# Second attention of a two-block layer: the softmax weights are divided on GpSimd before they are transposed, and the output is written in channel order

## The chip, the cores and the metric

The kernel runs on one core of a Trainium2 chip. The metric is the device time of one execution in microseconds (us); lower is better. The engines are named as the profile names them: PE (TensorE matmul), PEld (TensorE weight load), DVE (VectorE), ACT (ScalarE), POOL (GpSimd), SP (SyncE).

## What is computed

A model of two blocks in float32 over 1024 tokens. The first block (attention, two state-space mixers, a feed-forward part) is untouched. The second block projects the normed input into queries (8 heads of 64), keys and values (2 heads of 64), a gate, and a gated second branch. The part that changes is its attention:

```
def one_block(q_blk):
    s = jnp.einsum('bhgqd,bhkd->bhgqk', q_blk, kt).astype(jnp.float32) * scale
    p = jax.nn.softmax(s, axis=-1).astype(vt.dtype)
    return jnp.einsum('bhgqk,bhkd->bhgqd', p, vt)
...
attn = block_attention(q, k, v) * jax.nn.silu(gate_a)
y_a = jnp.einsum('bse,ed->bsd', attn, w_proj_attn)
```

Queries go in 8 blocks of 128, four query heads share a key head, and `scale` is 1/8. Each query sees all 1024 keys.

## The kernel before

Every engine has its own program, and all of them walk one list, `schedule`, which fixes each engine's order; semaphores tie the engines together. float32 products are made exact enough by splitting an operand into a rounded part (hi) and the rest (low).

The second attention is one stretch of that list, from 1475 to 1698 us of the profile. Its unit is a **pair** of query heads in one block of 128 tokens: 8 blocks times 4 pairs, 32 pairs. For head-block n (64 of them, two for each pair m):

- `a2s`: PE makes the scores, 128 queries by 1024 keys, in two PSUM banks (L1686). DVE takes the row maximum (L2800) and multiplies it by -0.125 (L2801).
- `a2e`: ACT makes exp(0.125 x - 0.125 max) of the 1024 columns into one of four SBUF tiles `Pb`, with the row sum into `a2d` (L2152). The weights stay undivided.
- `a2x (m, q)`, q = 0 to 3: PE transposes a quarter of both heads' `Pb` into a side bank (4 transposes, L1695), ACT copies it to the hi part of `PT` (L2161), DVE makes the low part (L2244).
- `a2v (m, q)`: PE multiplies the quarter with the values, hi and low stacked on the 128 partitions (L1707). After q = 3 ACT copies the sum to `ovt` (L2167).
- `a2o m`: `fold` is two identities side by side. Two products with `ovt` as the stationary operand (L1719) add hi and low and give the output with the queries on the partitions. DVE inverts the two row sums (L2810) and multiplies the output with them into `ot` (L2812).
- `a2t c`, after every fourth pair: PE transposes the four 128-column pieces of `ot` (L1725), and DVE copies them to the channel-major `aoT` (L2816).

The stages of neighbouring pairs are interleaved: `a2x (m+1, 0)` and `(m+1, 1)` stand between the value products of pair m. POOL has no work in the stretch. In front of it stand the query blocks (`q2T`, `q2B`: rotation and norm on DVE, where the gains in `qkg` are folded into the rotation table) and the making of `fold` (L2779); behind it come the gate product on DVE (L2819), sums of activations (`c2`) and the next projections (`vi`).

PE's side products share four banks in turn. A result of each DVE instruction is waited for before the next one of that engine runs; the helper `step` does this on ACT and POOL too.

## Time and profile before

| | |
|---|---|
| median of 3 runs | 2219.86 us (2218.81 to 2220.01) |
| the profiled execution, its own time | 2217.14 us |
| its span | 2215.3 us |
| PE, PEld busy | 94%, 79% of the span |
| DVE, ACT, POOL busy | 59%, 43%, 45% |
| granted TensorE clock, mean | 0.98 of full speed |

The page's 40 slices of some 55 us show the second attention as slices 27 to 31:

```
DVE  4443605867348734434479696789997865225532
POOL 1333433543336788888830302210002469885344
GB/s 153 73 104 113 144 51 49 72 120 63 147 58 96 39 58 60 67 65 76 67 181 143 143 93 122 82 29 1 1 1 34 39 20 58 114 96 105 105 124 76
```

A digit is the busy share of a slice in tenths. The shares of the whole span mix stages with different limits; what the change touches is read from its own stretch. Times in a timeline are counted from the start of the span.

### The profile page before, as it was taken

How to read it: one execution, taken by the hardware profiler on the slowest of the kernel's cores; microseconds unless marked ns; L12 is line 12 of the kernel's file. 1: busy time of each engine (PE TensorE's matmuls, PEld its weight loads, DVE VectorE, ACT ScalarE, POOL GpSimd, SP SyncE). 2: the span in 40 equal slices, each digit the busy share in tenths (PEclk: the TensorE clock that was granted, in tenths of full speed). 3: DMA queues.
4: the chain of work that ended last, by engine and by line, in shares of the span. 5: the costliest groups of instructions: out<-in, count | busy, mean ns of one | idle time of the engine just before them, and what ended most of it. 6: DMA issues, size and time to landing. Idle time of an engine off the chain costs nothing. (4 is left out here: it accounts for less than half of the span.)

```text
span 2215.3 us, 30029 instructions
## 1 busy us (share of the span) xinstructions
PE 2084.4 (94%) x10653; PEld 1750.5 (79%) x10661; DVE 1303.4 (59%) x1945; ACT 947.8 (43%) x1679; POOL 991.2 (45%) x723
## 2 busy tenths in 40 slices
PE   6999999889998999999999978989999999999997
PEld 6888877778786788888888857768887888887886
DVE  4443605867348734434479696789997865225532
ACT  4332215565234433343455544247775444544012
POOL 1333433543336788888830302210002469885344
PEclk9999999999999999999999999999999999999999
DMA  4233412354512122222254423210001102333331
GB/s 153 73 104 113 144 51 49 72 120 63 147 58 96 39 58 60 67 65 76 67 181 143 143 93 122 82 29 1 1 1 34 39 20 58 114 96 105 105 124 76
DMA packets 185892, 179.49 MB, mean 81 GB/s; under 512 B 27556, under 2 KB 147088, under 8 KB 184336
## 3 DMA queue, kind: packets, MB, share of 16 engines
q1 hardware_dynamic: 157568, 107.51, 16.7%
q10 hardware_dynamic: 19216, 46.99, 5.7%
q0 software_dynamic: 8960, 23.07, 4.7%
q8 instruction: 86, 1.41, 0.3%
q14 instruction: 62, 0.51, 0.1%
HBM read 150.81 MB, written 49.81 MB: 91 GB/s over the span
## 5 line engine op out<-in xcount | busy, mean ns | idle before, releaser
L1206 POOL TENSOR_SCALAR w_hi<-w_raw 128x1024 fp32r<-128x1024 f32 x67 | 76.2, 1137 | 469.3 <-issue 310.0
L1348 PE MATMUL gemm<-h_hi,w_hi 128*128 128x512 f32 x688 | 271.8, 395 | 5.6 <-POOL h_lo L1260 5.6
L1350 PE MATMUL gemm<-h_hi,w_lo 128*128 128x512 f32 x688 | 268.2, 390 | 0.0
L1349 PE MATMUL gemm<-h_lo,w_hi 128*128 128x512 f32 x688 | 268.0, 390 | 0.0
L954 POOL TENSOR_TENSOR w_lo<-wsum,w_hi 128x512 fp32r<-128x512 f32 x160 | 214.7, 1342 | 102.6 <-ACT w_hi L1814 94.7
L1814 ACT ACTIVATE w_hi<-wsum 128x512 fp32r<-128x512 f32 x171 | 108.3, 633 | 183.9 <-POOL wsum L945 94.1
L954 POOL TENSOR_TENSOR w_lo<-w_raw,w_hi 128x512 fp32r<-128x512 f32 x86 | 116.3, 1353 | 138.7 <-ACT w_hi L1814 134.1
L1209 POOL TENSOR_TENSOR w_lo<-w_raw,w_hi 128x1024 fp32r<-128x1024 f32 x67 | 166.8, 2489 | 5.6
L1430 PE MATMUL gemm<-h_hi,w_hi 128*128 128x512 f32 x416 | 161.9, 389 | 0.0
L1431 PE MATMUL gemm<-h_lo,w_hi 128*128 128x512 f32 x416 | 161.8, 389 | 0.0
L1432 PE MATMUL gemm<-h_hi,w_lo 128*128 128x512 f32 x416 | 161.8, 389 | 0.0
L1348 PEld LDWEIGHTS gemm<-h_hi,w_hi 128*128 128x128 f32 x688 | 129.4, 188 | 34.2 <-issue 8.7
L1350 PEld LDWEIGHTS gemm<-h_hi,w_lo 128*128 128x128 f32 x688 | 129.3, 188 | 27.4
L1349 PEld LDWEIGHTS gemm<-h_lo,w_hi 128*128 128x128 f32 x688 | 129.5, 188 | 25.4
L945 POOL TENSOR_TENSOR wsum<-w_raw,w_raw 128x512 f32<-128x512 f32 x96 | 129.3, 1347 | 7.5
L1255 POOL TENSOR_TENSOR wt<-h_lo 128x512 f32<-128x512 f32 x12 | 18.9, 1574 | 232.9 <-DVE aoT L2819 228.1
L2275 DVE SCALAR_TENSOR_TENSOR cacc<-cin,cols,cacc 128x1024 f32<-128x1024 f32 x42 | 65.5, 1560 | 84.5 <-ACT cacc L1773 83.5
L2341 DVE TENSOR_TENSOR ca<-m,gemm 128x512 f32<-128x512 f32 x32 | 22.0, 687 | 146.4 <-ACT m L1883 146.4
L1814 ACT ACTIVATE w_hi<-w_raw 128x512 fp32r<-128x512 f32 x130 | 82.3, 633 | 48.9 <-PE gemm L1432 36.6
L1430 PE MATMUL gemm<-cmb,w_hi 128*128 128x512 f32 x240 | 94.1, 392 | 4.2 <-POOL w_lo L954 4.2
L2161 ACT ACTIVATE PT<-side 128x512 fp32r<-128x512 f32 x128 | 76.6, 599 | 43.6 <-PE side L1695 39.3
L2244 DVE TENSOR_TENSOR PT<-side,PT 128x512 fp32r<-128x512 f32 x128 | 88.5, 691 | 9.7 <-ACT PT L2161 5.8
(487 smaller groups left out, 5425.2 us busy)
## 6 DMA issues: line engine op xcount, KB each, us to landing
w_raw<-in_w_in SPq DMA_DIRECT2D x60, 512.0 KB, 3.9
down_sums<-in_ffn_w_down POOLq DMA_DIRECT2D x24, 768.0 KB, 7.2
w_raw<-in_ffn_w_gate SPq DMA_DIRECT2D x22, 512.0 KB, 3.9
w_raw<-in_ffn_w_up SPq DMA_DIRECT2D x22, 512.0 KB, 4.0
w_raw<-down_sums SPq DMA_DIRECT2D x44, 256.0 KB, 2.7
w_raw<-in_ffn_w_down SPq DMA_DIRECT2D x44, 256.0 KB, 2.8
w_raw<-in_w_out SPq DMA_DIRECT2D x16, 512.0 KB, 3.8
sig_spill<-quad ACTq DMA_DIRECT2D x5, 1024.0 KB, 3.8
```

Of the source, the lines that this page charges most:

```text
L945: step(ops.tensor_tensor(wsum[sum_of[n]["buf"]][:], x, y, op), "w_sum" if who == "pool" else "w_sum_v")
L954: ops.tensor_tensor(quarter(wlo, slot), x, quarter(whi, slot), ALU.subtract).then_inc(w_split, 1)
L1209: gp.tensor_tensor(lo[:], raw[key % 4][:], hi[:], ALU.subtract).then_inc(w_split, 1)
L1348: mm(o, hi[:, k, m], act[0][:, k, t], start=k == 0, stop=False)
L1349: mm(o, hi[:, k, m], act[1][:, k, t], start=False, stop=False)
L1350: last = mm(o, lo[:, k, m], act[0][:, k, t], start=False, stop=k == kt - 1)
L1430: mm(o, hi[:, k, :], b[0], start=k == 0, stop=False)
L1431: mm(o, hi[:, k, :], b[1], start=False, stop=False)
L1432: last = mm(o, lo[:, k, :], b[0], start=False, stop=k == 3)
L1814: step(af(quarter(whi, slot), x, ACT.Copy), "w_quarter_hi")
L2161: step(af(PT[q][0][:], b[:], ACT.Copy), "hi_ready")
L2244: ins = v.tensor_tensor(dst, b, hi, ALU.subtract)
```

## The change

- POOL multiplies each `Pb` tile in place by the inverse of its row sum, a column of `a2d` (64 instructions of 128x1024, new kind `a2e` in POOL's program). The inverse is made by DVE with one instruction for each head-block (`weight_scale`). PE's transposes of a pair wait for POOL's product of its second head instead of ACT's exponentials.
- `fold` is 64 columns wide and is now the stationary operand, `ovt` the moving one: each of the two products writes 64 output partitions, and the output comes out in channel order. DVE copies 128 columns straight into `aoT`. L2810 and L2812 go, and `a2t` goes with its transposes and copies.
- The query gain in `qkg` is multiplied by -0.125 once. The scores are then the negated scaled ones, DVE takes their minimum (one instruction, no L2801), and ACT computes exp(-x + min). The bias columns rotate over four instead of two.

Waits that named the last `a2t` now name the last `a2o`. Unused semaphores go, which changes no instruction.

```diff
-        s += [("a2t", m // 4 - 1)] * (m % 4 == 0 and m > 0) + [("a2o", m)]
-    s += [("a2t", NT - 1), ("load", 3)]
+        s.append(("a2o", m))
+    s.append(("load", 3))
...
-        fold = sbuf("fold", [P], 216)
+        fold = sbuf("fold", [64], 216)
...
-        ot = sbuf("ot", [512], 212)
...
-                        side_consumed(pool, (("a2t", NT - 1), 0))
+                        side_consumed(pool, (("a2o", 4 * NT - 1), 0))
                         pool.wait_ge(N["ga_gated"], 1)
                     if j >= 2:
                         pool.wait_ge(N["c2_s"], j - 1)
                     step(gp.tensor_tensor(wt[j % 2][:], hF[1][:, r1, t1], hF[1][:, r2, t2], op), "c2_w")
+                elif kind == "a2e":
+                    pool.wait_ge(N["p_scale"], j + 1)
+                    step(gp.tensor_scalar(Pb[j % 4][:], Pb[j % 4][:], a2d[:, j % 8:j % 8 + 1], None, ALU.mult), "p_normed")
                 elif kind == "norm" and j[0] == 1:
...
-                        scores_consumed(pe, 2 * m)
-                        scores_consumed(pe, 2 * m + 1)
+                        pe.wait_ge(N["p_normed"], 2 * m + 2)
...
-                        last = mm(b[:, hslice(i)], ovt[j % 2][:, hslice(i)], fold[:], start=True, stop=True)
-                    done(last, (it, 0))
-                elif kind == "a2t":
-                    side_consumed(pe, (("a2o", 4 * j + 3), 0))
-                    b = bank((it, 0))
-                    for i in range(4):
-                        last = tr(b[:, hslice(i)], ot[:, hslice(i)], ident)
+                        last = mm(b[64 * i:64 * i + 64, 0:P], fold[:], ovt[j % 2][:, hslice(i)], start=True, stop=True)
                     done(last, (it, 0))
...
-                    step.frees_scores(af(Pb[j % 4][:], g[:], ACT.Exp, bias=a2m[:, 2 + j % 2:3 + j % 2], scale=0.125,
+                    step.frees_scores(af(Pb[j % 4][:], g[:], ACT.Exp, bias=a2m[:, j % 4:j % 4 + 1], scale=-1.0,
                                          accum_out=a2d[:, j % 8:j % 8 + 1]), j)
...
+            def weight_scale(n):
+
+                if n < 2 * 4 * NT:
+                    scores_consumed(dve, n)
+                    d = a2d[:, n % 8:n % 8 + 1]
+                    step(v.reciprocal(d, d), "p_scale")
+
...
+                            step(v.tensor_scalar(g, g, -0.125, None, ALU.mult))
...
-                        for k in range(2):
-                            step(v.tensor_copy(fold[r, 64 * k:64 * k + 64], ident[r, r]), "fold_ready" if h and k else None)
+                        step(v.tensor_copy(fold[r, :], ident[r, r]), "fold_ready" if h else None)
...
-                    mx, neg = a2m[:, j % 2:j % 2 + 1], a2m[:, 2 + j % 2:3 + j % 2]
-                    step(v.reduce_max(mx, g[:], axis=AX))
-                    step(v.tensor_scalar(neg, mx, -0.125, None, ALU.mult), "a2_max")
+                    step(v.tensor_reduce(a2m[:, j % 4:j % 4 + 1], g[:], axis=AX, op=ALU.min), "a2_max")
                 elif kind == "a2x":
-                    q = j[1]
+                    m, q = j
+                    if j == (0, 0):
+                        weight_scale(0)
+                        weight_scale(1)
+                    if q == 2:
+                        weight_scale(2 * m + 3)
                     b = side_product(dve, (it, 0))
                     low(PT[q][1][:], b[:], PT[q][0][:], (it, 0))
+                    if q == 0:
+                        weight_scale(2 * m + 2)
                 elif kind == "a2o":
-                    h = 2 * j % 8
-                    for i in range(2):
-                        scores_consumed(dve, 2 * j + i)
-                    step(v.reciprocal(a2r[:], a2d[:, h:h + 2]))
                     b = side_product(dve, (it, 0))
-                    step.frees(v.tensor_tensor(h64(ot[:, h * 64:h * 64 + P]), b[:, 0:256].rearrange("p (h n) -> p h n", h=2)[:, :, 0:64],
-                                               widen(a2r[:], 64), ALU.mult), (it, 0))
-                elif kind == "a2t":
-                    b = side_product(dve, (it, 0))
-                    step.frees(v.tensor_copy(aoT[:, :, hslice(j)], b[:].rearrange("p (i n) -> p i n", i=4)), (it, 0))
+                    step.frees(v.tensor_copy(aoT[:, j % 4, hslice(j // 4)], b[:, 0:P]), (it, 0))
```

What that does to the order. DVE, in the middle of the stage, over a little more than one pair (`PT_1` is the low part, `PT_0` the hi part; the number behind is a buffer). Before:

```order
L2800 TENSOR_REDUCE a2m<-gemm 128x1 [waits gemm_done1,side_read0]
L2801 TENSOR_SCALAR a2m<-a2m 128x1 [waits dve_step]
L2244 TENSOR_TENSOR PT_1_275<-side,PT_0_274 128x512 [waits hi_ready,side_done1,a2_max]
L2244 TENSOR_TENSOR PT_1_277<-side,PT_0_276 128x512 [waits hi_ready,side_done2,side_read1]
L2800 TENSOR_REDUCE a2m<-gemm 128x1 [waits gemm_done3,side_read2]
L2801 TENSOR_SCALAR a2m<-a2m 128x1 [waits dve_step]
L2810 RECIPROCAL a2r<-a2d 128x2 [waits gemm_read1,gemm_read3,a2_max]
L2812 TENSOR_TENSOR ot<-side,a2r 128x128 [waits side_done3,dve_step]
L2244 TENSOR_TENSOR PT_1_279<-side,PT_0_278 128x512 [waits hi_ready,side_done0,side_read3]
L2244 TENSOR_TENSOR PT_1_281<-side,PT_0_280 128x512 [waits hi_ready,side_done2,side_read0]
```

After:

```order
L2801 TENSOR_REDUCE a2m<-gemm 128x1 [waits gemm_done1,side_read1]
L2239 TENSOR_TENSOR PT_1_275<-side,PT_0_274 128x512 [waits hi_ready,side_done2,a2_max]
L2295 RECIPROCAL a2d<-a2d 128x1 [waits gemm_read3,side_read2]
L2239 TENSOR_TENSOR PT_1_277<-side,PT_0_276 128x512 [waits hi_ready,side_done3,p_scale]
L2801 TENSOR_REDUCE a2m<-gemm 128x1 [waits gemm_done3,side_read3]
L2815 COPY aoT<-side 128x128 [waits side_done0,a2_max]
L2295 RECIPROCAL a2d<-a2d 128x1 [waits gemm_read1,side_read0]
L2239 TENSOR_TENSOR PT_1_279<-side,PT_0_278 128x512 [waits hi_ready,side_done1,p_scale]
L2239 TENSOR_TENSOR PT_1_281<-side,PT_0_280 128x512 [waits hi_ready,side_done3,side_read1]
L2801 TENSOR_REDUCE a2m<-gemm 128x1 [waits gemm_done1,side_read3]
```

What was L2244, L2800 and L2812 is now L2239, L2801 and L2815. The multiplications of the maximum are gone, one inverse stands behind the low part of quarter 0 and one ahead of the low part of quarter 2, each waiting for ACT's exponential (gemm_read), and the product with the inverse has become a copy.

DVE at the start of the stage, from the third row reduction on. Before:

```order
L2800 TENSOR_REDUCE a2m<-gemm 128x1 [waits gemm_done3,a2_max]
L2801 TENSOR_SCALAR a2m<-a2m 128x1 [waits dve_step]
L2800 TENSOR_REDUCE a2m<-gemm 128x1 [waits gemm_done1,a2_max]
L2801 TENSOR_SCALAR a2m<-a2m 128x1 [waits dve_step]
L2244 TENSOR_TENSOR PT_1_275<-side,PT_0_274 128x512 [waits hi_ready,side_done1,a2_max]
L2244 TENSOR_TENSOR PT_1_277<-side,PT_0_276 128x512 [waits hi_ready,side_done2,side_read1]
```

After:

```order
L2801 TENSOR_REDUCE a2m<-gemm 128x1 [waits gemm_done3,a2_max]
L2801 TENSOR_REDUCE a2m<-gemm 128x1 [waits gemm_done1,a2_max]
L2295 RECIPROCAL a2d<-a2d 128x1 [waits gemm_read3,a2_max]
L2295 RECIPROCAL a2d<-a2d 128x1 [waits gemm_read1,p_scale]
L2239 TENSOR_TENSOR PT_1_275<-side,PT_0_274 128x512 [waits hi_ready,side_done1,p_scale]
L2295 RECIPROCAL a2d<-a2d 128x1 [waits gemm_read3,side_read1]
L2239 TENSOR_TENSOR PT_1_277<-side,PT_0_276 128x512 [waits hi_ready,side_done2,p_scale]
```

The first two inverses stand behind the fourth row reduction, and with them all that follows from them.

POOL at the same place. Before:

```order
L1206 TENSOR_SCALAR w_hi_55<-w_raw_53 128x1024 [waits raw_loaded2,gemm_done1,w_split]
L1209 TENSOR_TENSOR w_lo_57<-w_raw_53,w_hi_55 128x1024 [waits pool_hi]
L1255 TENSOR_TENSOR wt_294<-h_lo 128x512 [waits ga_gated,side_read0,w_split]
L1255 TENSOR_TENSOR wt_295<-h_lo 128x512 [waits c2_w]
```

After (`Pb` in place, with a column of `a2d`):

```order
L1205 TENSOR_SCALAR w_hi_55<-w_raw_53 128x1024 [waits raw_loaded2,gemm_done1,w_split]
L1208 TENSOR_TENSOR w_lo_57<-w_raw_53,w_hi_55 128x1024 [waits pool_hi]
L1257 TENSOR_SCALAR Pb_270<-Pb_270,a2d 128x1024 [waits p_scale,w_split]
L1257 TENSOR_SCALAR Pb_271<-Pb_271,a2d 128x1024 [waits p_scale,p_normed]
L1257 TENSOR_SCALAR Pb_272<-Pb_272,a2d 128x1024 [waits p_scale,p_normed]
L1257 TENSOR_SCALAR Pb_273<-Pb_273,a2d 128x1024 [waits p_scale,p_normed]
```

Between the last split of weights and the first sum (`wt`) now stand 64 in-place products.

## Rows read from the trace of the kernel before

**Rows 1.** Windows view: busy us of PE, PEld, DVE, ACT, POOL, clock, DMA, GB/s

```profile
1475.00:1698.00 223.00, 205.72 (x1445) 182.12 (x1446) 196.92 (x330) 167.39 (x289) 0.00 (x0) 0.98 0.01 1
1482.00:1485.00 3.00, 3.00 (x8) 2.35 (x9) 1.07 (x1) 1.10 (x2) 0.00 (x0) 0.52 0.00 0
```

**Rows 2.** Groups by shape, DVE, 1490-1690 us: count, busy us, mean ns, idle before

```profile
L2244 DVE TENSOR_TENSOR PT<-side,PT 128x512 fp32r<-128x512 f32 x124 | 85.7, 691 | 7.6 <-ACT PT L2161 3.7
...
L2800 DVE TENSOR_REDUCE a2m<-gemm 128x1 f32<-128x1024 f32 x60 | 73.5, 1224 | 2.0
...
L2801 DVE TENSOR_SCALAR a2m<-a2m 128x1 f32<-128x1 f32 x60 | 9.2, 153 | 2.1
L2812 DVE TENSOR_TENSOR ot<-side,a2r 128x128 f32<-128x128 f32 x30 | 8.7, 291 | 1.3 <-DVE a2r L2810 0.2 <-PE side L1719 0.2
L2810 DVE RECIPROCAL a2r<-a2d 128x2 f32<-128x2 f32 x30 | 5.0, 166 | 1.0
L2816 DVE COPY aoT<-side 128x512 f32<-128x512 f32 x7 | 4.8, 691 | 0.2
```

**Rows 3.** Timeline, DVE: start us, length us, engine, line, instruction, count

```profile
1559.03 1.42 DVE L2244 TENSOR_TENSOR PT<-side,PT 128x512 fp32r<-128x512 f32 x2
```

**Rows 4.** ACT's copy of a pair's output: all 32 (ns min/median/max), and the second

```profile
L2167 ACT ACTIVATE ovt<-side x32: 384/386/388, 1494.0 to 1694.9; 128x256 f32<-128x256 f32 x32
...
1500.10 0.39 ACT L2167 ACTIVATE ovt<-side 128x256 f32<-128x256 f32 x1
```

**Rows 5.** POOL instructions by line: one SBUF input, then two inputs

```profile
L1206 POOL TENSOR_SCALAR w_hi<-w_raw x67: 1034/1053/4873, 11.4 to 2181.1; 128x1024 fp32r<-128x1024 f32 x67
...
L1285 POOL TENSOR_TENSOR xc<-xs,dts 128x512 f32<-128x512 f32 x8 | 8.4, 1046 | 11.0 <-DVE SQ L2679 10.4
```

**Rows 6.** Timeline: POOL beside DVE, at 231 us and at 1467 us

```profile
231.42 4.43 DVE L2632 TENSOR_TENSOR psq<-qkv 128x4096 f32<-128x4096 f32 x1 [0.21 <-DVE da L2579]
...
231.89 4.87 POOL L1206 TENSOR_SCALAR w_hi<-w_raw 128x1024 fp32r<-128x1024 f32 x1 [7.15 <-PE gemm L1350]
...
1467.81 1.05 POOL L1206 TENSOR_SCALAR w_hi<-w_raw 128x1024 fp32r<-128x1024 f32 x1 [10.76 <-issue]
```

**Rows 7.** Timeline: hand-overs between engines

```profile
330.08 1.04 POOL L1273 TENSOR_TENSOR md<-con,da 128x512 f32<-128x512 f32 x1
...
331.17 0.30 PEld L1558 LDWEIGHTS side<-md,con 128*128 128x128 f32 x2 [2.71 <-POOL md L1273]
...
1549.03 0.42 PEld L1695 LDWEIGHTS side<-con,Pb 128*128 128x128 f32 x4 [1.56 <-DVE aoT L2816]
...
1549.81 0.60 ACT L2161 ACTIVATE PT<-side 128x512 fp32r<-128x512 f32 x1 [1.89 <-PE side L1695]
...
1550.54 0.69 DVE L2244 TENSOR_TENSOR PT<-side,PT 128x512 fp32r<-128x512 f32 x1 [0.31 <-ACT PT L2161]
...
1697.99 1.22 DVE L2819 TENSOR_TENSOR aoT<-aoT,gaT 128x1024 f32<-128x1024 f32 x1
...
1699.38 2.99 POOL L1255 TENSOR_TENSOR wt<-h_lo 128x512 f32<-128x512 f32 x2 [228.08 <-DVE aoT L2819]
```

**Rows 8.** Timeline: start of the stage

```profile
1471.34 0.86 DVE L2779 COPY fold<-con 64x64 f32<-64x64 f32 x4
...
1484.90 0.23 PEld L1695 LDWEIGHTS side<-con,Pb 128*128 128x128 f32 x1
...
1485.63 1.23 DVE L2800 TENSOR_REDUCE a2m<-gemm 128x1 f32<-128x1024 f32 x1 [0.29 <-PE gemm L1686]
```

**Rows 9.** End of the stage, and a product of 64 output rows, 128 passes

```profile
1690.39 0.52 PEld L1719 LDWEIGHTS side<-fold,ovt 128*128 128x128 f32 x4 [0.97 <-ACT ovt L2167]
...
1695.33 0.52 PEld L1719 LDWEIGHTS side<-fold,ovt 128*128 128x128 f32 x4 [0.76 <-ACT ovt L2167]
...
1696.88 0.19 PEld L1348 LDWEIGHTS gemm<-h_hi,w_hi 128*128 128x128 f32 x1
...
L1735 PE MATMUL side<-wsT,vv x128: 272/273/323, 1794.0 to 1807.1; 128*64 128x128 f32 x128
```

More of the change, by code:

```diff
@@ L339, in products_of @@
     return list(range({"cols": 1, "norm": 8, "mx": 8, "smT": 1, "acs": 1, "convT": 2, "zT": 2, "avT": 2, "q2T": 2, "q2B": 4, "v2T": 2, "viT": 2, "ln": 2, "a2x": 1, "a2v": 0 if kind != "a2v" or a[1] else 1, "a2o": 1,
-                       "a2t": 1, "sp": 1, "c3": 1, "ly": 1, "uw": 1, "pa": 1, "sg": 1, "yo": 1, "yd": 1, "st": 1, "r1": 1, "r2": 1,
+                       "sp": 1, "c3": 1, "ly": 1, "uw": 1, "pa": 1, "sg": 1, "yo": 1, "yd": 1, "st": 1, "r1": 1, "r2": 1,
                        "ap": 2, "ao": 1}.get(kind, 0)))
@@ L715, in build_program @@
             "init_done", "masks_ready", "md_ready", "ss_ready", "diag_ready", "hi_ready", "conv_acc", "conv_act", "sm_abs", "sm_exp", "inv_done", "x_exp",
-            "sm_arg", "beta_ready", "da_ready", "eacs_ready", "prep_done", "att_max", "att_exp", "rec_kb",
+            "sm_arg", "da_ready", "eacs_ready", "att_max", "att_exp", "rec_kb",
             "rec_vn", "rec_S", "mix_ssd", "mix_gdn", "gated", "sq_gdn", "kbv_ready", "resid_done", "d_hi", "d_low", "d_sum", "d_used", "d_copied", "w_sum_v", "rope_done", "gb_used",
             "mean_done", "ln_done", "a2_max", "split_hi", "split_lo", "y_done", "yT_hi", "yT_lo", "final_done",
-            "ga_gated", "pt_used", "fold_ready", "tok_sq", "kx_ready", "ed_ready", "o_summed", "sq_ssd",
+            "ga_gated", "pt_used", "fold_ready", "p_normed", "p_scale", "tok_sq", "kx_ready", "ed_ready", "o_summed", "sq_ssd",
             "ssd_rs", "gdn_rs", "pool_step", "sq_part", "rs_ready",
-            "ln_sq", "c2_w", "c2_s", "c2_hi", "c2_lo", "idr_ready", "quad_ready", "vm_used",
+            "ln_sq", "c2_w", "c2_s", "c2_hi", "c2_lo", "idr_ready", "quad_ready",
             "low_ready", "acc_gained", "comb_sum", "comb_add", "comb_hi", "comb_lo", "w_sum", "w_quarter_hi", "t_copied", "sg_ready", "f_made", "tok_used", "ob_sq", "ob_gained")}
@@ L1980, in _ @@
                     act.wait_ge(N["sm_arg"], 1)
-                    step(af(beta[:], sm[3][:, :, 8:12], ACT.Exp), "beta_ready")
+                    step(af(beta[:], sm[3][:, :, 8:12], ACT.Exp))
                     side_consumed(act, (it, 0))
@@ L2110, in _ @@
                     elif j == 3:
-                        side_consumed(act, (("a2t", NT - 1), 0))
+                        side_consumed(act, (("a2o", 4 * NT - 1), 0))
                         side_product(act, (("a2v", (NT * 4 - 1, 0)), 0))
@@ L2183, in _ @@
                     if j == 0:
-                        side_consumed(act, (("a2t", NT - 1), 0))
+                        side_consumed(act, (("a2o", 4 * NT - 1), 0))
                     act.wait_ge(N["c2_s"], j + 1)
@@ L2311, in mixed @@
                 x = uT[:, q, 512 * t:512 * t + 512].rearrange("p (c n) -> p c n", c=4)
-                step(v.tensor_tensor(x, x, vm[:, 4 * t:4 * t + 4, q, :], ALU.mult), "vm_used")
+                step(v.tensor_tensor(x, x, vm[:, 4 * t:4 * t + 4, q, :], ALU.mult))
             def gates(n, i):
@@ L2640, in _ @@
                     step(v.memset(akT[:], 0.0))
-                    step(v.memset(av[:, 0, :], 0.0), "prep_done")
+                    step(v.memset(av[:, 0, :], 0.0))
                 elif kind == "as":
```

## The prediction

> **What bounds the kernel now.** I first read the slices of the page: the change lies in slices 27 to 31, where POOL and the DMA engines stand still. The windows view of that stretch [rows 1] gives PE 205.7 and DVE 196.9 of 223 us busy, ACT 167.4, POOL 0. Two engines are close to full, so shares decide nothing. The groups by shape [rows 2] let me count DVE's work for one pair: 2 reductions of 1.224, 2 scalings of the maximum of 0.153, 4 low parts of 0.691, one inverse of 0.166 and one product of 0.291, together 5.975 us. Two low parts in a row take 1.42 [rows 3], so 0.035 lies between instructions; ten of these make 6.33 us a pair. Each fourth pair adds a copy of 0.691 + 0.035 = 0.73. Over 31 pairs with 7 such copies that is 31 x 6.33 + 7 x 0.73 = 201.3 us. ACT's copy of a pair's output runs from 1494.0 to 1694.9, which is 200.9 us for 31 intervals [rows 4]. **DVE sets the pace.** PE alone can do a pair in 6.1 us: that is the first interval, 1494.0 to 1500.1, before DVE has fallen behind [rows 4]. PE's wait of 1.56 us for DVE's `aoT` copy [rows 7] is the backlog becoming visible at the only place where PE needs a late DVE result.
>
> **What the change does to a pair.** On DVE the two scalings go (-0.306), the inverse of two columns becomes two of one column (+0.166; I take 0.166 for each, between nothing added and twice that), and the product becomes a copy of the same 128 columns from PSUM (0.291 kept; the 512-column copy took 0.691, the same as the 512-column low part, so the kind of operation does not show). The minimum is priced as the maximum. That is 5.835 us in 9 instructions, with gaps 6.15. The copy each fourth pair goes altogether. PE's pair loses nothing by name, but the fold is now two products with 64 output rows. The nearest row, also 64 rows out and 128 columns moving, ran 128 passes in 1807.1 - 1794.0 = 13.1 us, 0.10 each [rows 9]; four passes take 0.41 where they took 0.52, so PE could do a pair in 6.0. ACT does what it did.
>
> **The new loop.** DVE now releases POOL, POOL releases PE, PE releases ACT, and ACT releases DVE, within one pair. I followed it once around, from the low part of quarter 0 of one pair to that of the next. DVE: low part 0.691, inverse 0.166, low part 0.691, reduction 1.224, copy 0.291, inverse 0.166, with five gaps 3.40. DVE to POOL: DVE's end at 1699.21 to POOL's start at 1699.38, 0.17. Then POOL's product, P. POOL to PE: 331.12 to 331.17, 0.05. PE's transposes until ACT starts: 1549.03 to 1549.81, 0.78. ACT's copy 0.60. ACT to DVE: 1550.41 to 1550.54, 0.13 [rows 7]. Together **5.13 + P**. With P = 1.05 the loop takes 6.18 and DVE's own work 6.15: the change puts a latency loop exactly as long as the engine it relieves. Each 0.1 us more in P then costs 0.1 us a pair, about 3 us in all. Behind PE's new wait are queued the transposes and value products that DVE, ACT and the next output need; behind DVE's new waits for an exponential stand its low parts, which PE waits for.
>
> **The price of P.** No row shows POOL scaling a tile with a column of factors. Nearest below: one SBUF input, 1024 columns, constant factors, 1.034 at the least and 1.053 in the median of 67 [rows 5]. Far above: two SBUF inputs with a broadcast one, 512 columns, 1.046 [rows 5], so at most 2.09 for 1024. I take 1.10, close to the first, because the instruction is the same TENSOR_SCALAR of the same shape and only has to fetch one column more. Both ends stay for the range.
>
> The Trainium skill, page "GPSIMD Engine Reference", section "Performance pitfalls for Q7 kernels", gives about 102 cycles for a read command that does not pipeline with the one before; at the page's 1.2 GHz that is an estimate of 0.085 us for the fetch of the column. By it P would be 1.14 and the result about 1.2 us worse than my sum.
>
> **The sum,** against the profiled execution. *Body:* with P = 1.10 a pair takes 6.23. The last two pairs have no scores left and no division of their own to wait for: the last interval before was 1695.33 - 1690.39 = 4.94 [rows 9], and I leave both at that. 29 x 6.23 + 2 x 4.94 = 190.6 against 200.9: **-10.3**. *Start:* PE began the transposes at 1484.90, directly behind the scores [rows 8]. Now the fourth reduction (start 1485.63, end 1486.86), an inverse (1487.06), the hand-over 0.17, two POOL products of 1.10 and 0.05 come before them: about 1489.5, **+4.6**. Nothing hides that, since PE, ACT and DVE all wait for the first transposes. *Clock:* behind the wait for the first exponentials PE ran at a granted 0.52, the 1.2 GHz level, from 1482 to 1485 [rows 1]. The new wait, 1485.6 to 1489.5, is at least as long as that one, so I expect it again. If the next 3 us ran at that level and all waited for PE, it would cost 1.5; part is covered by ACT's exponentials, and I take **+0.8** (0 to 1.5). *End:* fold, inverse product, transposes back and only then the next projection, 1695.33 to 1696.88, 1.55 us [rows 9]; now the projection follows the fold's 0.41: **-1.1**. DVE's last copy of 0.69 goes too, but PE has the next projection by then. *Before the stage:* DVE works without a break up to the first scores. One instruction of 64 columns is added and two of the four `fold` copies go, 0.86 / 4 = 0.215 each [rows 8]: **-0.2**. POOL's other work, the weight splits and `c2`, stands in front of and behind the 64 products, and POOL is idle 228 us there [rows 7], so the products themselves (64 x 1.1 = 70 us) take nobody's time. No DMA moves.
>
> -10.3 + 4.6 + 0.8 - 1.1 - 0.2 = **-6.2 us**. The profiled execution would go from 2217.1 to 2210.9; the median of the runs stands 2.7 above it, so from 2219.9 to **2213.7**. What follows the stage is PE's, which passes the gain on.
>
> **Rivals.**
>
> *Slower: POOL is the loop.* If the factor column makes POOL treat the product as a two-input operation, P is up to 2.09, the loop 7.22, and 29 pairs cost 28.7 us more than in my sum, the start 2.0 more: -6.2 + 30.7 = +24.5, 2244 us. It decides from P = 1.10 + 6.2/31 = 1.30 on: at that value the gain is gone, at 1.44 the change is 0.2% slower. For it: no row shows the form. Against it: the row with one SBUF input. Chance of the whole band above 1.44: 0.18.
>
> *No change to speak of.* P between 1.16 and 1.44, or hand-overs a little longer than the single ones I read: the gain on DVE is real, and the loop and the start give it back. Within 4.4 us (0.2%, about what a measurement of this kernel can tell from no change), centre 2218. Chance 0.25.
>
> *Contention.* POOL's constant-factor product took 4.87 us at 231.89, beside a DVE product of two SBUF tensors that ran until 235.85; yet at 1467.81, beside DVE's low parts, it took 1.05 [rows 6]. In this stage no DVE instruction has two SBUF tensors. Were the low parts held up all the same, by half a POOL product each time, 64 x 0.55 = 35 us would be lost. I give it 0.02. The rule behind it is in the Trainium skill, "SBUF — State Buffer", section "Who interferes with whom": a DVE instruction with two SBUF inputs and a GpSimd one that reads SBUF exclude each other, the later one waits for all of the earlier. The trace at 231 us agrees (4.87 against 1.05); whether it spares the low parts over a whole stage only the run will tell.
>
> *More gain.* If P is 1.04 and clock and start cost nothing beyond the POOL products, DVE's 6.15 is the pace: -8.5 to -10, 2210 us. Chance 0.07. *The change misses its aim:* DVE's second inverse waits for an exponential that comes late, so DVE idles in front of it. ACT has 167.4 / 32 = 5.2 us of work in a pair of 6.2 [rows 1], so some slack is there; I count it in the case of no change.
>
> **How the numbers follow.** My case (P 1.04 to 1.16, 2210 to 2216 us) has 0.48. With the case of more gain, faster by over 0.2% has 0.55, within 0.2% 0.25, slower 0.20. The range leaves out the contention and the upper half of the POOL rival: 2209 to 2229 us; its upper end is P = 1.6.
>
> **What would show it.** Right: DVE's scaling of the maximum and the wait for `aoT` are gone, POOL's 64 products take 1.05 to 1.15, ACT's output copies come every 6.2 us without a longer interval each fourth pair, the first transposes start some 4.6 us after they did, with a low granted clock behind them. Wrong in the sum: intervals of 6.5 or more with PE waiting for POOL (the loop), low parts longer than 0.70 (contention), or DVE idle before its inverses.

## The result, and the profile after

| | before | changed |
|---|---|---|
| median of 4 runs | 2219.94 us (2218.81 to 2220.59) | 2296.52 us (2295.01 to 2297.21) |
| the profiled execution, its own time; its span | 2217.14; 2215.3 | 2296.62; 2294.8 |
| granted clock, mean | 0.98 | 0.97 |

The ratio is 1.0343, 95% interval [1.0327, 1.0359]: **3.4% slower**, 76.6 us, where the prediction had 6.2 us less. Its range ended at 2229.

POOL's products explain it almost alone. These are PE's and POOL's busy slices on the page of the changed kernel (57 us each now; slices 27 to 30 lie wholly in the stage, which begins late in slice 26 and ends with slice 31), and the group of the products (count, busy us, mean ns, idle before):

```profile
PE   6999999889998999999999889777777999999997
...
POOL 1333433434336888888502122266665649886334
...
L1257 POOL TENSOR_SCALAR Pb<-Pb,a2d 128x1024 f32<-128x1024 f32 x64 | 182.2, 2847 | 110.7 <-DVE a2d L2295 108.8
```

PE stands at 7 in every slice of the stage. POOL stands at 6 in slices 27 to 30 and at 5 in slice 31.

One product takes **2.85 us**. The row the price was read from has 1.053 [rows 5]. ACT's copy of a pair's output (line, ns min/median/max, first and last start) answers to [rows 4]:

```profile
L2162 ACT ACTIVATE ovt<-side x32: 384/385/387, 1504.4 to 1774.7; 128x256 f32<-128x256 f32 x32
```

That is 31 intervals in 270.3 us, where before had 200.9. The stage's windows (as [rows 1]; here POOL is busy, so its column is not zero):

```profile
1475.00:1778.00 303.00, 228.38 (x1419) 187.29 (x1420) 189.17 (x292) 167.41 (x289) 182.74 (x65) 0.89 0.01 2
1492.00:1500.00 8.00, 6.55 (x25) 5.67 (x26) 3.63 (x6) 4.20 (x7) 3.92 (x3) 0.50 0.00 1
```

PE is busy 228 of 303 us and POOL only 183. No engine is full: this is a loop of waits. The waits view of 1490 to 1750 us (total, times, longest) shows it as a ring, in which each engine waits for the one before it:

```profile
ACT PT L2156 <- PE side L1696: 108.4, 99, 10.8
POOL Pb L1257 <- DVE a2d L2295: 89.5, 41, 3.5
PEld side L1696 <- POOL Pb L1257: 75.9, 30, 8.3
DVE PT L2239 <- ACT PT L2156: 75.4, 44, 7.8
```

DVE's wait for ACT was 3.7 us in [rows 2]. PE's wait for `aoT` is gone, as the change meant. One turn of the ring, from the timeline:

```profile
1610.25 0.16 DVE L2295 RECIPROCAL a2d<-a2d 128x1 f32<-128x1 f32 x1
...
1610.58 5.79 POOL L1257 TENSOR_SCALAR Pb<-Pb,a2d 128x1024 f32<-128x1024 f32 x2 [2.61 <-DVE a2d L2295]
...
1616.42 0.66 PE L1696 MATMUL side<-con,Pb 128*128 128x128 f32 x4 [2.18 <-POOL Pb L1257]
...
1617.20 0.60 ACT L2156 ACTIVATE PT<-side 128x512 fp32r<-128x512 f32 x1 [2.38 <-PE side L1696]
...
1617.93 0.69 DVE L2239 TENSOR_TENSOR PT<-side,PT 128x512 fp32r<-128x512 f32 x1 [2.27 <-ACT PT L2156]
...
1618.98 2.85 POOL L1257 TENSOR_SCALAR Pb<-Pb,a2d 128x1024 f32<-128x1024 f32 x1 [2.61 <-DVE a2d L2295]
```

**This is not the loop of the prediction.** There, only the second product of a pair lies between DVE's inverse and PE. Here POOL runs both back to back: the second inverse (1612.76 to 1612.92) was ready 0.5 us before the first product's end. The turn is low part 0.69, a gap of 0.03, inverse 0.17, hand-over to POOL 0.17, *two* products and 0.08 between them, POOL to PE 0.05, transposes until ACT starts 0.78, ACT's copy 0.60, ACT to DVE 0.13: **2.70 + 2P**, 8.40 with P = 2.85, and POOL's starts stand 1618.98 - 1610.58 = 8.40 apart. The pair takes the larger of 5.13 + P and 2.70 + 2P; they cross at P = 2.43.

The very last interval has no product in it. It took 4.92 or 4.93 us in the six kernels below that have the new fold, so 30 x 8.40 + 4.92 = 256.9 us are accounted for. The other 13.4 us are clock. Here are three starts of ACT's copy and one group of transposes between them, then three windows in a row:

```profile
1618.74 0.39 ACT L2162 ACTIVATE ovt<-side 128x256 f32<-128x256 f32 x1
...
1627.14 0.39 ACT L2162 ACTIVATE ovt<-side 128x256 f32<-128x256 f32 x1
...
1633.22 1.12 PE L1696 MATMUL side<-con,Pb 128*128 128x128 f32 x4 [2.15 <-POOL Pb L1257]
...
1636.95 0.39 ACT L2162 ACTIVATE ovt<-side 128x256 f32<-128x256 f32 x1 [0.19 <-PE side L1708]
```

```profile
1622.10:1630.80 8.70, 6.54 (x47) 5.23 (x45) 6.12 (x10) 5.50 (x10) 6.00 (x3) 1.00 0.00 0
1630.80:1639.50 8.70, 6.54 (x39) 5.65 (x38) 4.74 (x8) 4.21 (x8) 5.22 (x2) 0.80 0.00 0
1639.50:1648.20 8.70, 7.06 (x52) 5.87 (x51) 6.54 (x11) 5.76 (x10) 5.71 (x3) 1.00 0.01 2
```

A pair is 8.40 us at full clock, and 9.81 where the window's clock is 0.80: PE waited 2.15 us for POOL, the clock was 0.50 (the 1.2 GHz level) from 1634 to 1636, and four transposes took 1.12 instead of 0.66. The next pair takes 8.05, so this one costs 1.06 net. Of 28 such windows in a row, 1500 to 1744 us, 11 have 0.80 or 0.81; at 1.06 each that is 11.7 us, and the 27 intervals that end by 1742.8 are 11.6 longer than 27 x 8.40. Most of the rest is the last interval, 6.42 instead of 4.92 at a mean clock of 0.62.

Against the profile of before, the difference splits by four marks (the first transposes, the first and the last output copy, the end): start 1492.3 - 1484.9 = +7.4; from there to the first copy 12.1 against 9.1, +3.0; body 270.3 - 200.9 = +69.4; the rest 520.1 against 520.4, -0.3. The sum, 79.5, is the difference of the spans.

What remained open: why 2.85 and not 1.05? Candidates were the column of factors, writing in place, the instruction's form, and contention. Contention is out already: all 64 products lie between 2844 and 2853 ns, and the first two ran from 1486.48 to 1492.27 while DVE did nothing (its inverses end at 1486.50, its next instruction starts at 1494.26). And do the prediction's other terms hold once P is small?

### The profile page after: what moved, and what is told of

It is laid out like the page before. It is cut to its first block and busy times, and to the rows that moved or that the text cites. A ratio compares the mean times of both kernels' runs of the same rounds, so it can differ in the third digit from the quotient of the medians.

```text
span 2294.8 us, 30068 instructions
## 1 busy us (share of the span) xinstructions
PE 2110.1 (92%) x10621; PEld 1757.9 (77%) x10629; DVE 1292.1 (56%) x1904; ACT 947.8 (41%) x1679; POOL 1172.6 (51%) x787
## 5 line engine op out<-in xcount | busy, mean ns | idle before, releaser
L1257 POOL TENSOR_SCALAR Pb<-Pb,a2d 128x1024 f32<-128x1024 f32 x64 | 182.2, 2847 | 110.7 <-DVE a2d L2295 108.8
L1696 PE MATMUL side<-con,Pb 128*128 128x128 f32 x512 | 89.9, 304 | 68.1 <-POOL Pb L1257 68.1
L2239 DVE TENSOR_TENSOR PT<-side,PT 128x512 fp32r<-128x512 f32 x128 | 88.5, 691 | 91.1 <-ACT PT L2156 86.9
L1696 PEld LDWEIGHTS side<-con,Pb 128*128 128x128 f32 x512 | 63.0, 152 | 87.7 <-POOL Pb L1257 81.9
```

The source lines that it names most:

```text
L1257: step(gp.tensor_scalar(Pb[j % 4][:], Pb[j % 4][:], a2d[:, j % 8:j % 8 + 1], None, ALU.mult), "p_normed")
L1696: last = tr(b[:, hslice(i)], Pb[(2 * m + i % 2) % 4][:, hslice(2 * q + i // 2)], ident)
```

## The experiments

### A constant instead of the column

```diff
-                    step(gp.tensor_scalar(Pb[j % 4][:], Pb[j % 4][:], a2d[:, j % 8:j % 8 + 1], None, ALU.mult), "p_normed")
+                    step(gp.tensor_scalar(Pb[j % 4][:], Pb[j % 4][:], 1.0, None, ALU.mult), "p_normed")
```

> The changed kernel with one operand of POOL's 64 products exchanged: the constant 1.0 in place of the column of inverses (so the weights stay undivided; every wait and every DVE inverse is kept). Theory 'column': the per-partition factor is what makes POOL's product take 2.85 us; with a constant it takes 1.05, the loop 5.13 + 1.05 = 6.18 us a pair, and the kernel comes out where the prediction put it, 2211 to 2216 us. Rival 'form': the in-place float32 result or the single operation (the fast weight split has two constant operations and an fp32r result) is slow, whatever the factor; then the product stays at 2.85 and the time at about 2296 us.

Measured: 2289.31 us (2287.18 to 2291.08; before 2218.55 on the same chip, for this run and the next two), ratio 1.0317 [1.03, 1.0334]. From its page:

```profile
L1257 POOL TENSOR_SCALAR Pb<-Pb 128x1024 f32<-128x1024 f32 x64 | 177.3, 2770 | 109.4 <-DVE a2d L2295 107.6
```

The column costs 0.077 us (2.847 against 2.770 in the mean). It is not what makes the product slow.

This run also bears out the second loop. With P = 2.77 it gives 2.70 + 5.54 = 8.24 us, the first 5.13 + 2.77 = 7.90. Two intervals of ACT's copy, one at full clock and one not, as windows:

```profile
1610.13:1618.37 8.24, 6.23 (x45) 5.10 (x44) 5.84 (x10) 5.19 (x10) 5.54 (x2) 1.00 0.00 1
1618.37:1627.93 9.56, 7.57 (x44) 6.48 (x43) 6.02 (x11) 5.18 (x9) 6.32 (x3) 0.82 0.01 3
```

### Two tensors instead of a scalar form

```diff
-                    step(gp.tensor_scalar(Pb[j % 4][:], Pb[j % 4][:], a2d[:, j % 8:j % 8 + 1], None, ALU.mult), "p_normed")
+                    step(gp.tensor_tensor(Pb[j % 4][:], Pb[j % 4][:], a2d[:, j % 8:j % 8 + 1].to_broadcast([P, T]), ALU.mult), "p_normed")
```

> The changed kernel with POOL's product written as a TENSOR_TENSOR of the tile and the column broadcast over 1024 columns; nothing else changes, the result is the same. Theory 'form of instruction': two-input products with a broadcast operand took 1.04 us for 512 columns before, so at most 2.09 for 1024; the pair then takes the larger of 5.13 + 2.09 = 7.2 and 2.70 + 2 x 2.09 = 6.9 us, the body 29 x 7.2 = 209 instead of 261 us, the start 1.5 us less: 2240 to 2250 us if the clock stays up. Rival 'any per-partition factor costs POOL 2.8 us': no change, about 2296 us.

Measured: 2237.21 us (2236.02 to 2239.45), ratio 1.0085 [1.007, 1.01]. The forecast of 2240 to 2250 stood on a product of 2.09.

```profile
L1257 POOL TENSOR_TENSOR Pb<-Pb,a2d 128x1024 f32<-128x1024 f32 x64 | 121.2, 1893 | 115.1 <-DVE a2d L2295 114.9
```

and the view of the output copies:

```profile
L2162 ACT ACTIVATE ovt<-side x32: 383/385/385, 1501.7 to 1716.1; 128x256 f32<-128x256 f32 x32
```

The same product over a broadcast input takes 1.89 us, *less* than the one-input form, so neither the in-place write nor the amount of data is the cause. Of the 31 intervals 28 lie between 6.98 and 7.00, where the first loop gives 5.13 + 1.89 = 7.02 and the second 6.49. The last but one takes 6.46 and the last 4.92.

### No products on POOL at all

```diff
-                        pe.wait_ge(N["p_normed"], 2 * m + 2)
+                        scores_consumed(pe, 2 * m)
+                        scores_consumed(pe, 2 * m + 1)
```

and the products and the inverses are left out, so the output stays undivided.

> The changed kernel without the division: POOL's products and DVE's inverses are left out, PE's transposes wait for ACT's exponentials again; the fold in channel order and the negated scale stay (the output is undivided). Theory 'only the POOL loop is bad': DVE has 2 x 1.224 + 4 x 0.691 + 0.291 and 7 gaps = 5.75 us a pair, PE 6.0, so PE sets the pace; 29 x 6.0 + 2 x 4.9 = 184 against 200.9 us, with the end -1.1: 2200 to 2204 us. Rival 'the new fold or the waits of the transposes cost something of their own': intervals above 6.2 us and a time above 2208.

Measured: 2199.08 us (2197.85 to 2200.41), ratio 0.9912 [0.9897, 0.9927]. That is 0.9 below the forecast. The copies come from 1492.1 to 1676.8; 29 intervals lie between 6.01 and 6.04, PE's pace, where 6.0 was expected. So what the changed kernel loses comes through the inverses, the products and the waits for them, and from nothing else in the change.

### Eight forms of the product in one kernel

In this kernel `r` is the column `a2d[:, j % 8:j % 8 + 1]` and `f` is `j // 8`:

```diff
+                    if f == 1:
+                        ins = gp.tensor_scalar(x, x, 1.0, None, ALU.mult)
+                    elif f == 2:
+                        ins = gp.tensor_scalar(x, x, 1.0, 0.0, ALU.mult, ALU.add)
+                    elif f == 3:
+                        ins = gp.tensor_scalar(x, x, r, 0.0, ALU.mult, ALU.add)
+                    elif f == 4:
+                        ins = gp.tensor_tensor(x, x, r.to_broadcast([P, T]), ALU.mult)
...
```

> The changed kernel with eight forms of POOL's product, eight tiles each, in this order: column factor in place (as it is); one constant operation in place; two constant operations in place; column factor and a second constant operation; TENSOR_TENSOR with the broadcast column; column factor on 512 of the 1024 columns; column factor, source another tile; one constant operation, source another tile (output wrong from the second group on). Theory 'column': 2.85, 1.05, 1.05, 2.85, 2.1, half of 2.85 plus a fixed part (1.5), 2.85, 1.05. Rival 'in place': 2.85 in the first five, 1.05 in the last two. Rival 'single operation': only the third and the fourth are fast.

Measured: 2260.79 us, one run. Each line is one form, eight times (ns min/median/max): the column and one operation; a constant and one operation; a constant and a second constant operation; **the column and a second constant operation**; the broadcast; 512 columns of the first; the first and the second with another tile as source.

```profile
L1274 POOL TENSOR_SCALAR Pb<-Pb,a2d x8: 2842/2844/2847, 1488.1 to 1518.6; 128x1024 f32<-128x1024 f32 x8
...
L1260 POOL TENSOR_SCALAR Pb<-Pb x8: 2769/2770/2772, 1524.1 to 1552.5; 128x1024 f32<-128x1024 f32 x8
...
L1262 POOL TENSOR_SCALAR Pb<-Pb x8: 1044/1049/1059, 1557.9 to 1580.7; 128x1024 f32<-128x1024 f32 x8
...
L1264 POOL TENSOR_SCALAR Pb<-Pb,a2d x8: 1118/1126/1132, 1584.4 to 1605.7; 128x1024 f32<-128x1024 f32 x8
...
L1266 POOL TENSOR_TENSOR Pb<-Pb,a2d x8: 1893/1893/1894, 1609.4 to 1632.9; 128x1024 f32<-128x1024 f32 x8
...
L1268 POOL TENSOR_SCALAR Pb<-Pb,a2d x8: 1563/1564/1567, 1637.4 to 1659.9; 128x512 f32<-128x512 f32 x8
...
L1270 POOL TENSOR_SCALAR Pb<-h_lo,a2d x8: 2842/2844/2847, 1664.1 to 1693.3; 128x1024 f32<-128x1024 f32 x8
...
L1272 POOL TENSOR_SCALAR Pb<-h_lo x8: 2769/2771/2775, 1699.2 to 1727.5; 128x1024 f32<-128x1024 f32 x8
```

**A second operation makes the instruction 2.5 times faster**, although it asks for more: 1.126 against 2.844 with the column, 1.049 against 2.770 with a constant. Reading from another tile, so not in place, changes nothing. Of the three cases only 'single operation' foresaw this. The trace calls all of them but the broadcast TENSOR_SCALAR.

### Is it any single operation?

```diff
+                    if f == 1:
+                        ins = gp.tensor_scalar(x, x, 0.0, None, ALU.add)
+                    elif f == 2:
+                        ins = gp.tensor_scalar(x, x, -1.0, None, ALU.max)
+                    elif f == 3:
+                        ins = gp.tensor_scalar(x, x, r, 1.0, ALU.mult, ALU.mult)
+                    elif f == 4:
+                        ins = gp.tensor_scalar(x, x, 1.0, r, ALU.mult, ALU.mult)
+                    elif f == 5:
+                        ins = gp.tensor_scalar(Pb[j % 4][:, 0:512], Pb[j % 4][:, 0:512], r, 0.0, ALU.mult, ALU.add)
+                    elif f == 6:
+                        ins = gp.tensor_copy(x, hF[1][:, 0, :])
+                    elif f == 7:
+                        ins = gp.tensor_scalar(Pb[j % 4][:, 0:512], Pb[j % 4][:, 0:512], 1.0, None, ALU.mult)
...
```

> The changed kernel with eight forms of POOL's instruction in turn, eight head-blocks each, so its output is not the attention's: (0) the column, one operation, as the control; (1) a constant, one operation, add; (2) a constant, one operation, max; (3) the column, then times the constant 1.0; (4) times the constant 1.0, then the column; (5) the column and plus 0.0 on 512 columns; (6) a plain copy of 1024 columns; (7) a constant, one operation, 512 columns. Theory 'any single operation is slow': (1) and (2) take 2.77 us like the multiplication, (3) and (4) 1.12 to 1.13, (5) 0.6 to 0.65, (7) about 1.5. Rival 'only the lone multiplication is slow, or adding a zero constant has a fast path of its own': (1) and (2) take 1.05 us, or (3) and (4) take 2 us and more. The pair intervals give no new information; the time should lie between those of the kernel with the short product and the changed kernel, 2225 to 2270 us.

Measured: 2244.57 us, one run; the lines in the order of the edit:

```profile
L1260 POOL TENSOR_SCALAR Pb<-Pb x8: 2769/2770/2787, 1522.8 to 1551.6; 128x1024 f32<-128x1024 f32 x8
...
L1262 POOL TENSOR_SCALAR Pb<-Pb x8: 2764/2765/2774, 1556.9 to 1587.1; 128x1024 f32<-128x1024 f32 x8
...
L1264 POOL TENSOR_SCALAR Pb<-Pb,a2d x8: 1117/1124/1130, 1592.8 to 1615.2; 128x1024 f32<-128x1024 f32 x8
...
L1266 POOL TENSOR_SCALAR Pb<-Pb,a2d x8: 1119/1126/1137, 1619.0 to 1640.2; 128x1024 f32<-128x1024 f32 x8
...
L1268 POOL TENSOR_SCALAR Pb<-Pb,a2d x8: 687/692/700, 1644.0 to 1664.9; 128x512 f32<-128x512 f32 x8
...
L1270 POOL COPY Pb<-h_lo x8: 1036/1042/1049, 1668.5 to 1689.5; 128x1024 f32<-128x1024 f32 x8
...
L1272 POOL TENSOR_SCALAR Pb<-Pb x8: 1488/1489/1496, 1693.1 to 1714.7; 128x512 f32<-128x512 f32 x8
```

Multiplication, addition and maximum alone are all slow; the second operation may be an addition or a multiplication, and the column may stand first or second. (5) is 0.69 where 0.60 to 0.65 was expected, so a part of the time does not shrink with the columns. Between 512 and 1024 columns one operation costs (2.844 - 1.564) / 512 = 2.50 ns a column, two cost (1.126 - 0.692) / 512 = 0.85 ns. Why POOL takes so much longer over one operation is not shown.

### The changed kernel with the short form

```diff
-                    step(gp.tensor_scalar(Pb[j % 4][:], Pb[j % 4][:], a2d[:, j % 8:j % 8 + 1], None, ALU.mult), "p_normed")
+                    step(gp.tensor_scalar(Pb[j % 4][:], Pb[j % 4][:], a2d[:, j % 8:j % 8 + 1], 0.0, ALU.mult, ALU.add), "p_normed")
```

> The changed kernel, with POOL's product written with a second constant operation (times the column, plus 0.0): the same values in another form of the same instruction. Theory 'form': POOL's product takes 1.12 to 1.13 us instead of 2.85, the loop 5.13 + 1.126 = 6.26 a pair, and the prediction's own sum then holds: body 29 x 6.26 + 2 x 4.94 = 191.4 against 200.9, -9.5; start +4.6, clock +0.8, end -1.1, before the stage -0.2: -5.4, so 2213 to 2216 us. Output copies every 6.2 to 6.3 us. Rival 'the other terms of the prediction are wrong as well' (two products in a row, the half clock after waits, hand-overs in the whole stage): 2218 or more although the product is short.

Measured: **2214.21 us** (2213.25 to 2216.36, 10 runs), before 2219.43 on the same chip, for this run and the next three; ratio 0.9978 [0.9969, 0.9987]. A second, neutral operation in one instruction turns 3.4% slower into 0.2% faster.

```profile
L1257 POOL TENSOR_SCALAR Pb<-Pb,a2d 128x1024 f32<-128x1024 f32 x64 | 71.9, 1124 | 140.7 <-DVE a2d L2295 140.6
```

and the views of the copies and of the first transposes:

```profile
L2162 ACT ACTIVATE ovt<-side x32: 383/384/385, 1500.6 to 1692.7; 128x256 f32<-128x256 f32 x32
```

```profile
1489.32 1.97 PE L1696 MATMUL side<-con,Pb 128*128 128x128 f32 x8 [4.10 <-POOL Pb L1257]
```

By the four marks: first transposes 1489.3 - 1484.9 = +4.4; from there to the first copy 11.3 against 9.1, +2.2; body 192.1 against 200.9, -8.8 (most intervals are 6.25, the last but one is 5.54, the last 4.92); the rest 519.3 against 520.4, -1.1. Sum -3.3, as the spans 2212.0 and 2215.3 have it. The profiled execution of before was itself a quick one (2217.14, 2.3 under the median of this chip's 14 runs of it), which accounts for most of what the medians, 5.2 apart, show beyond that.

### The first inverses earlier

```diff
                 elif kind == "a2s":
...
+                    if j in (2, 3):
+                        weight_scale(j - 2)
...
                     if j == (0, 0):
-                        weight_scale(0)
-                        weight_scale(1)
```

> As e6_two, and DVE makes the first two inverses in front of its third and fourth row minimum, instead of behind the fourth, so that POOL can divide the first pair of weight tiles while PE still makes scores. Nothing else moves. Theory 'the start costs what the prediction said': the first transposes come again directly behind the fourth scores or within 1 us of it, 4 to 4.6 us earlier than in e6_two, and PE's low clock at the start of the transposes goes, 0 to 1.5: 4 to 6 us less than e6_two, 2208 to 2211 us. Rival: the inverses wait for exponentials that are late, so DVE's third and fourth minimum and with them the fifth and sixth scores are late, and most of it is lost again: less than 2 us gained.

Measured: 2211.99 us (2209.74 to 2212.76), ratio 0.9964 [0.9951, 0.9978]: 2.2 less, not 4 to 6. From PE's second group of scores to the first transposes it is 1487.67 - 1483.60 = 4.07 us, in the kernel above 1489.32 - 1482.00 = 7.32. So 3.25 of 4.33 came back (before: 1484.90 - 1481.91 = 2.99); the second inverse stands behind the third minimum, ends at 1486.32, and POOL's product after it is the wait that is left. The scores themselves came 1.60 us later in this profile than in the kernel above (1483.60 against 1482.00). The two kernels do not differ before them, the runs of one kernel lie 3 to 4 us apart, and the cause was not looked for. The clock term stayed: 0.51 in 1485 to 1492, and 11.3 us again from the transposes to the first copy (1499.0). So the forecast was nearly right about the transposes (1.03 us behind the end of the fourth scores) and wrong about the clock. The rival did not occur: DVE's third minimum still starts 1.30 us after PE begins these scores, as above.

### The second inverse ahead of the output's copy

```diff
+                    if j == (0, 2):
+                        weight_scale(3)
-                    if q == 2:
-                        weight_scale(2 * m + 3)
...
                 elif kind == "a2o":
+                    weight_scale(2 * j + 5)
```

on top of the edit above.

> As e7_start, and the inverse of a pair's second head stands in front of DVE's copy of the output of the pair before (a2o) instead of in front of the low part of quarter 2. The copy's 0.291 + 0.035 leaves the loop: 5.13 - 0.33 + 1.126 = 5.93 us, under DVE's own 6.15. Theory 'loop': DVE's work becomes the pace, 6.15 instead of 6.26 a pair, about 3 us less than e7_start, 2205 to 2208 us. Rival 'ACT's exponential of the second head is not there yet when DVE comes to the inverse': DVE idles in front of the inverse, and nothing is gained or 1 to 3 us are lost.

Measured: **2207.22 us** (2206.9 to 2207.96), ratio 0.9945 [0.9932, 0.9957]. The copies run from 1498.0 to 1686.6, 188.6 us, 3.5 less than with the other order, and the interval went from 6.25 to between 6.12 and 6.18 in most pairs. The loop alone would allow 5.93 and PE 6.02; DVE's own work is 6.15. So the loop is off the path, and DVE sets the pace. The time fell by 4.8 us; the profile's other 1.0 us is an earlier first copy, which the edit does not touch. This version beats both kernels.

### The negated scale alone

```diff
-  step(v.reduce_max(mx, g[:], axis=AX))
-  step(v.tensor_scalar(neg, mx, -0.125, None, ALU.mult), "a2_max")
+  step(v.tensor_reduce(a2m[:, j % 4:j % 4 + 1], g[:], axis=AX, op=ALU.min), "a2_max")
```

with the factor in `qkg` and the scale of ACT's exponential, on the kernel before.

> The kernel before with the negated scale alone: the query gain is multiplied by -0.125 once, DVE takes a minimum and no longer scales the maximum. Everything else stays (division after the fold, transposes back). DVE's pair loses two scalings of 0.153 us and their two gaps of 0.035, 0.38 in all, so 5.95 us of DVE against PE's own 6.1 (the first interval of the output copies before). Theory 'DVE sets the pace before': PE takes over at about 6.1 a pair; 31 x 6.1 plus at most 7 x 0.4 for the pairs with the transposes back is 189 to 192 instead of 200.9, and the first exponentials come 0.15 to 0.3 earlier: 8 to 11 us less, 2209 to 2212 us where before has 2219.9. Rival 'a latency loop, not DVE's work, set the pace before': the scaling is hidden in a wait, and the time changes by less than 2 us.

Measured: 2210.41 us (2209.45 to 2211.4), ratio 0.9959 [0.9946, 0.9971], 9.0 less. The copies run from 1496.2 to 1688.6: 192.4 against 200.9. The single intervals say where DVE's work was the limit. Before, most pairs took 6.06 to 6.32 us, and each fourth 8.0:

```profile
1518.85 0.39 ACT L2167 ACTIVATE ovt<-side 128x256 f32<-128x256 f32 x1
...
1526.87 0.39 ACT L2167 ACTIVATE ovt<-side 128x256 f32<-128x256 f32 x1
...
1532.93 0.39 ACT L2167 ACTIVATE ovt<-side 128x256 f32<-128x256 f32 x1
```

With the scalings gone most pairs take 6.06, as PE alone does, and each fourth 6.98. DVE's backlog of four pairs came due at the fourth, where PE waits for `aoT`; nearly the whole gain lies there (7 x 1.04 = 7.3 of 8.5 us). Each fourth pair still costs 0.9 more than the others, not the 0.4 that was allowed, so a part of that wait is not DVE's backlog: by DVE's work, 4 x 5.95 + 0.73 = 24.5 against PE's 4 x 6.06 = 24.2, only 0.3 would be. What the rest is was not looked for.

One small instruction fewer for each head-block on the engine that sets the pace is worth more than the whole change with the short product in its first order (-5.2). Against the kernel before on its own chip, the negated scale gives -9.0. With the channel order as well, and without any division, it is 2199.08 - 2218.55 = -19.5. The division on POOL then takes 14.3 of that back in the first order and 7.3 in the last (-12.2).

## Why the prediction was wrong, point by point

- **What bounds the kernel: held.** DVE set the pace over four pairs, not in each: three ran at PE's 6.06 to 6.3, and the backlog showed in the fourth, as the reading of the `aoT` wait had it. With the scalings alone gone, 31 x 6.1 and up to 2.8 gave 189 to 192; 192.4 was measured.
- **The price of P: this is the step that failed.** "I take 1.10, close to the first, because the instruction is the same TENSOR_SCALAR of the same shape and only has to fetch one column more." The name and the shape in the row were the same, the instruction was not: L1206 is written with two operations (times 1.0, plus 0.0), the new one with one. It was P = 2.85, above even the upper bound of 2.09. In the loop of the prediction that alone is 29 x (7.98 - 6.23) = 50.8 us of the 79.7 by which the body was missed. A two-input row is no upper bound for a one-input form. The fetch of the column was rightly priced: 0.077 (constant against column), where the sum took 0.05 (1.10 against 1.053).
- **The new loop: right in form, incomplete.** 5.13 + P gives 6.25 and 7.02 for P = 1.12 and 1.89; 6.25 and 7.00 were measured. The second loop, 2.70 + 2P, was missed, because only the second product was followed from DVE to PE. With P = 2.85 the first alone gives 7.98, so the miss is worth 0.42 x 29 = 12.2 us. And the last pair but one was not short: it waits for the last pair's products, which took it to 5.54 (P = 1.12) and 6.46 (P = 1.89) instead of 4.94. In the changed kernel, taken at 8.40, that is 3.5 us more. With 13.4 of clock the four terms make 79.9, against the 79.7 of the miss.
- **The break-even: fits.** 1.30 was named. P = 1.12 is faster by 5.2 us, P = 1.89 slower by 18.7. That is 31 us for each us of P, as the sum had it, and puts the break-even at 1.29, an estimate by straight line. No run stood between the two.
- **Start +4.6: held in size.** +4.4 with P = 1.12, and +7.4 with 2.85: two products of 1.73 more are 3.5, and DVE's inverses began 0.45 earlier in that profile (1486.14 against 1486.59), as did the whole stage.
- **Clock +0.8 (0 to 1.5): too small.** +2.2 in the kernel with the short product, where the granted clock was 0.50 (the 1.2 GHz level) from 1485 to 1496. In the changed kernel it was +3.0, of which 0.55 is PE's wait for the second pair's product at 1502.09 and not clock. The 13.4 us of low clock in the body stood in no term.
- **End -1.1, before the stage -0.2: the first held,** -1.1 from the last copy to the end (-0.3 in the changed kernel, whose clock was still low at the last copies); the second is below what the profiles can tell.
- **The sum at P = 1.126** was -5.4, and the medians differ by 5.2. Part of that is luck: the profiles differ by 3.3, with body +0.7 (0.6 of it the last pair but one) and clock +1.4 worse than their terms, and the rest as forecast.
- **The rivals.** "POOL is the loop" is what happened, with another cause and a larger price. It had 0.18 and ended at 2.09; it should have had no upper end from a different instruction. Contention did not occur. The Trainium skill, "SBUF — State Buffer", section "Who interferes with whom", says that a DVE instruction with at most one SBUF input, outside the two-port modes, does not contend with GpSimd. The trace agrees: 2844 to 2853 ns beside low parts of 691 ns, which have one input in PSUM.

The Trainium skill, "GPSIMD Engine Reference", section "Elementwise — side-by-side cycle accounting", gives 1.03 cycles an element for bodies of up to two operations. At its 1.2 GHz that is an estimate of 0.86 ns; the form with two operations shows 0.85 and agrees. The form with one shows 2.50, and the measurement decides.

## What to carry to other kernels

A duration from the trace is the price of an instruction as it is written, number of operations included: before taking a row for a new instruction, compare the two source lines, not only the name and the shape. Where one instruction comes twice in a loop, write one equation for each place at which the loop can be entered, and take the largest. When a change has several parts, price each alone: here the negated scale and the channel order gained, and the division on POOL cost at least 7.3 us of that in every form that was tried.

## What the runs showed of the hardware

- On POOL a TENSOR_SCALAR over 128x1024 float32 takes 2.77 us with one operation on a constant (mult, add or max) and 1.05 with two (mult, then add); a copy takes 1.04; a broadcast two-input product 1.89. So a second operation that does nothing pays: 64 x 1.72 us of POOL's time, and 82 us of this kernel's.
- A column of factors instead of a constant costs 0.075 us an instruction.
- With a wait of about 2.2 us for POOL in each pair, PE's granted clock was 1.00 in 17 of 28 windows of 8.7 us and 0.80 or 0.81 in 11, with no longer wait in the one that was followed closely (2.15); that one cost 1.06 us net. With P = 2.77 the long intervals (9.3 to 9.6 us) came every fourth pair from 1594 us on, and the others took 8.0 to 8.24. With the broadcast product (P = 1.89) the clock stayed at 1.00 from 1500 to 1690 us. What decides which pair is hit was not tried.
